# Delta heads of a hybrid decoder layer: order of decays, products, triangle and projections around the triangular inverse

## The chip, the cores and the metric

One core of a Trainium2 chip runs the whole program in one launch. The metric is device time in microseconds. The kernel before took 3432.81 us in the median of three runs (3431.79 to 3434.91).

## What is computed

The program is one inference step of one decoder layer, in float32: a SwiGLU block, a mixer with two branches, and a second SwiGLU block, for a prompt of 1024 tokens and for 8 sample sequences of 4 tokens (32 rows). Branch A is differential attention, branch B a gated DeltaNet. The change lies in branch B. Its core, by head, in chunks:

```python
gc = jnp.cumsum(g.reshape(B, H, n, C), axis=-1)
decay = jnp.exp(jnp.where(incl, gc[..., :, None] - gc[..., None, :], -jnp.inf))
kb = k * beta[..., None]
lower = jnp.where(strict, jnp.einsum('bhncd,bhnmd->bhncm', kb, k) * decay, 0.0)
sol = lax.linalg.triangular_solve(jnp.eye(C, dtype=q.dtype) + lower, rhs, left_side=True, lower=True)
qk = jnp.einsum('bhncd,bhnmd->bhncm', q, k) * decay
q_dec = q * jnp.exp(gc)[..., None]
# then per chunk:
v_new = u_i - w_i @ S
o_i = qd_i @ S + qk_i @ v_new
S = S * gt_i + kd_i.T @ v_new
```

Ahead of this, q, k and v are projected from the normed input, go through a causal convolution of width 4 and SiLU, and q and k are scaled to length one. Behind it, each output row is normed and multiplied by silu(z).

## The kernel before, in words

`delta_heads` (L1132) does branch B for 8 heads of 128 columns. It uses chunks of 128 tokens: 8 tiles of 128 tokens and one of the 32 sample rows (tile 8, called TT). Five instruction streams are written by hand, one per engine, each with its own function `head(h)`; semaphores join them. The order of the code is the order of the work on each engine. The heads run one after another, and the first, the inner and the last are the same code with small differences. The last head has no next head to project for: its "q" unit projects z, its other units project attention's output through the first columns of `w_a_out`, and its z units land in `acc_early`.

**Projections.** `piece(h, kind, c, i, of)` (L1984) is one third (352 columns) of a projection with 1024 inputs: 24 matmuls, as weights and inputs are split in a high and a low part and three of the products are kept. `i, of` cuts a piece in parts. The units of a head are q, z, k, v in this order; q, k and v are those of the next head, z of this one. ACT moves each piece out of PSUM in `take` (L1372), and makes the high part of weights in `high` (L1368); DVE makes the low part in `low` (L1592). `gather` (L1596) and three `product` (L1617) are the convolution on DVE, `silus` (L1409) its SiLU on ACT. PSUM banks 0 and 1 serve the pieces in turn.

**A head on TensorE**, in order: transposes of q and k by tile (`token`), with thirds of the last v piece between them and the transposes of the output rows of the head before (`out_rows`, L2054); piece q 0; `grams` 0 to 3 (L2091), which give k times q and k times k of each tile in banks 2 to 5; pieces q 1 and q 2; gram 4; piece z 0; then the inverse. This goes level by level, up to blocks of 128: in each level 1 to 5 the P products (L2126, in the fifth L2129) of two halves of four tiles, a filling `between(k)`, the R products (L2140), and a second filling. A filling is a sixth of a z piece, four matmuls. For levels up to 4 each P or R group is 64 matmuls of 32x32. Level 6 (`p_last`, `r_last`, L2150 to L2162) is 64x64. After it come value and key products and the scan over the 8 tiles (L2250 to L2261), filled with the k and v pieces.

**What feeds the inverse.** DVE takes the distances of the cumulative gates (`distances`, L1721; gc comes by DMA into `lo_t`, `load_gc` L1312). ACT takes their exponentials, from `qk_t` into `lo_t` (L1494). POOL multiplies by the triangle, from `lo_t` into `qk_t` (L1893). DVE multiplies by the grams in `products(t)` (L1732): first `lo_t`, the lower matrix (L1738), then `qk_t` (L1740), tile by tile. ACT cuts the 32x32 diagonal blocks into `lo_d` (L1504), POOL masks them by level (`masks`, L1897: L1906, L1909, L1913), DVE transposes (`base`, L1771) and TensorE begins. In each level ACT moves P out of PSUM (`moves`, L1512), DVE subtracts R (`update`, L1781) and transposes (`turned`). POOL writes the small blocks into the large matrix in `put` (L1915) and makes kp, scaled q (L1936) and kd ahead of it.

**Norm of the output rows** of the head before: ACT `out_root` (L1447), DVE `row_norm` (L1631), transposes on TensorE, `gate_rows` (L1640) with silu(z). The lengths of q and k: ACT `square`, DVE `sums` (L1703), ACT root (L1487), DVE `scale_columns` (L1708).

## Time and profile before

| | |
|---|---|
| median of three runs | 3432.81 us |
| the profiled execution | 3437.1 us, span of the core 3435.4 us |
| mean granted TensorE clock | 0.984 of full |
| TensorE (PE) busy | 96% |
| its weight loads (PEld) | 91% |
| DVE, ACT, POOL busy | 54%, 42%, 20% |
| DMA | 112 GB/s in the mean |
| the delta heads | from about 1668 to 2424 us |

PE is TensorE, DVE the vector engine, ACT the scalar engine, POOL GpSimd, SP the queue that issues most DMAs. A row of a timeline gives the start, the duration, the engine and line, what is written and read, how many were merged (x), and in brackets how long the engine was idle before it and which instruction ended that. "issue" is idle time in which the engine waited for nothing that the profile shows. PEclk is the clock that TensorE was granted; it has two levels, 1.2 GHz (0.50) and 2.4 GHz (1.00). Matmuls are pipelined, and their ends are modelled.

### The profile page before, as it was taken

Reading aid. Unit: us, or ns where it says so; the run is one execution under the profiler, and the core shown is the slowest. Engines: PE = TensorE matmul, PEld = TensorE weight load, DVE = VectorE, ACT = ScalarE, POOL = GpSimd, SP = SyncE. Lnnn points to the kernel's source line nnn. Section 1 sums busy time; section 2 is a strip of 40 time slices with the busy share of each in tenths; the row PEclk is TensorE's granted clock in tenths of the full one; section 3 lists DMA queues with packets and bytes.
Section 4 is the critical chain, followed back from the end, with each engine's and each line's share of the span. In section 5 each row is a group of like instructions: output and inputs, shape, how many; then the busy total and the mean of one; then the engine's idle time right before and its main releaser. Section 6 shows DMA issues by size and latency. Waiting matters only on the chain. (4 is left out here: it accounts for less than half of the span.)

```text
span 3435.4 us, 70539 instructions
## 1 busy us (share of the span) xinstructions
PE 3314.3 (96%) x28074; PEld 3136.1 (91%) x28074; DVE 1868.7 (54%) x3332; ACT 1459.7 (42%) x3057; POOL 696.4 (20%) x645
## 2 busy tenths in 40 slices
PE   7999999998999999999999999998999899999998
PEld 7999999997888888877788989988999899999998
DVE  6655565764555455544445555554441865556555
ACT  5222235555555555443344444444323722223444
POOL 2323310102122222000022222222001333221000
PEclk9999999999999999999999999999999999999999
DMA  5222236732222222389311111114522322224664
GB/s 165 75 78 84 82 121 218 234 124 70 69 69 69 70 69 69 121 305 379 106 42 44 52 51 52 52 51 130 164 81 75 119 81 82 75 75 147 201 195 141
DMA packets 351893, 385.45 MB, mean 112 GB/s; under 512 B 22492, under 2 KB 259110, under 8 KB 351422
## 3 DMA queue, kind: packets, MB, share of 16 engines
q1 hardware_dynamic: 341606, 347.78, 32.4%
q0 software_dynamic: 9888, 32.88, 2.7%
q8 instruction: 227, 3.72, 0.5%
q14 instruction: 88, 0.72, 0.1%
q10 hardware_dynamic: 84, 0.35, 0.0%
HBM read 305.53 MB, written 75.40 MB: 111 GB/s over the span
## 5 line engine op out<-in xcount | busy, mean ns | idle before, releaser
L673 PE MATMUL ps<-p_hi,w_hi 128*128 128x352 f32 x912 | 304.5, 334 | 2.3 <-PEq L123 1.4
L673 PE MATMUL ps<-p_hi,w_lo 128*128 128x352 f32 x912 | 294.1, 322 | 0.0
L673 PE MATMUL ps<-p_lo,w_hi 128*128 128x352 f32 x912 | 293.4, 322 | 0.0
L1999 PE MATMUL ps<-p_hi,w_hi 128*128 128x352 f32 x840 | 285.6, 340 | 0.0
L1999 PE MATMUL ps<-p_lo,w_hi 128*128 128x352 f32 x840 | 281.9, 336 | 0.2 <-issue 0.2
L1999 PE MATMUL ps<-p_hi,w_lo 128*128 128x352 f32 x840 | 280.8, 334 | 0.0
L673 PEld LDWEIGHTS ps<-p_hi,w_hi 128*128 128x128 f32 x912 | 172.2, 189 | 4.1 <-issue 1.7
L2840 PE MATMUL ps<-op_hid_hi,w_hi 128*128 128x384 f32 (+1 forms) x528 | 170.8, 324 | 4.1 <-DVE w_lo L2515 2.3
L2840 PE MATMUL ps<-f_hid_hi,w_hi 128*128 128x352 f32 x528 | 171.3, 325 | 1.6 <-DVE w_lo L2515 1.5
L673 PEld LDWEIGHTS ps<-p_lo,w_hi 128*128 128x128 f32 x912 | 172.6, 189 | 0.0
L673 PEld LDWEIGHTS ps<-p_hi,w_lo 128*128 128x128 f32 x912 | 171.7, 188 | 0.0
L2840 PE MATMUL ps<-f_hid_lo,w_hi 128*128 128x352 f32 x528 | 169.8, 322 | 0.0
L2840 PE MATMUL ps<-f_hid_hi,w_lo 128*128 128x352 f32 x528 | 169.7, 321 | 0.0
L2840 PE MATMUL ps<-op_hid_hi,w_lo 128*128 128x384 f32 (+1 forms) x528 | 169.4, 321 | 0.0
L2840 PE MATMUL ps<-op_hid_lo,w_hi 128*128 128x384 f32 (+1 forms) x528 | 169.3, 321 | 0.0
L1999 PEld LDWEIGHTS ps<-p_lo,w_hi 128*128 128x128 f32 x840 | 161.4, 192 | 2.6 <-issue 0.7
L1999 PEld LDWEIGHTS ps<-p_hi,w_hi 128*128 128x128 f32 x840 | 161.0, 192 | 2.6
L1999 PEld LDWEIGHTS ps<-p_hi,w_lo 128*128 128x128 f32 x840 | 161.3, 192 | 1.0
L2515 DVE TENSOR_TENSOR w_lo<-w_raw,w_hi 128x512 fp32r<-128x512 f32 x136 | 100.6, 747 | 87.2 <-ACT w_hi L2511 86.9
L414 ACT ACTIVATE at_prob<-ps,at_nmax 128x256 f32<-128x256 f32 (+7 forms) x128 | 94.4, 739 | 81.2 <-DVE at_nmax L520 79.5
L2511 ACT CAST w_hi<-w_raw 128x512 fp32r<-128x512 f32 x136 | 83.7, 619 | 106.2 <-PE ps L2840 106.0
L347 ACT ACTIVATE at_rotx<-ps 32x352 f32<-32x352 f32 x192 | 87.5, 456 | 89.1 <-DVE at_cosx L468 55.0
(698 smaller groups left out, 10354.8 us busy)
## 6 DMA issues: line engine op xcount, KB each, us to landing
w_raw<-in_ffn_w_out_dram SPq DMA_DIRECT2D x136, 256.0 KB, 3.4
w_raw<-in_w_in_dram SPq DMA_DIRECT2D x67, 512.0 KB, 4.0
sa_v<-in_cache_v_dram SPq DMA_DIRECT2D x120, 256.0 KB, 6.7
w_raw<-in_ffn_w_in_dram SPq DMA_DIRECT2D x48, 512.0 KB, 5.1
sa_k<-in_cache_k_dram SPq DMA_DIRECT2D x72, 256.0 KB, 5.5
f_s<-in_ffn_w_out_dram SPq DMA_DIRECT2D x64, 256.0 KB, 3.5
pair_s<-in_ffn_w_out_dram SPq DMA_DIRECT2D x64, 256.0 KB, 3.4
d_hid<-f_gb SPq DMA_DIRECT2D x44, 264.0 KB, 2.1
```

Of the source, the lines that this page charges most:

```text
L347: ins = nc.scalar.mul(dst, src, HD ** -0.5 if kind == "q" else 1.0)
L414: nc.scalar.activation(pr[:, i % 2, a, 0:(i + 1) * P], m.ps[:, 2 + 2 * a:4 + 2 * a, :].rearrange("p b k -> p (b k)")[:, 0:(i + 1) * P], AC ...
L673: mm = nc.tensor.matmul(m.ps[:, bank, 0:CH], a[:, k, w], b[:, f, cols(c)], start=(f == 0 and i == 0), stop=(f == KT - 1 and i == 2))
L1999: mm = nc.tensor.matmul(m.ps[:, (k + c) % 2, 0:CH], a[:, k, f * P:(f + 1) * P], x[:, f, cols(c)], start=(j == 0), stop=(j == len(terms) - 1))
L2511: nc.scalar.copy(unit_slot(u, False), unit_raw(u)).then_inc(e.out_hi, 1)
L2515: nc.vector.tensor_tensor(unit_slot(u, True), unit_raw(u), unit_slot(u, False).bitcast(F32), ALU.subtract).then_inc(e.out_lo, 1)
L2840: mm = nc.tensor.matmul(m.ps[:, bank, 0:hi - lo], unit_slot(u, low_part)[:, o * P:(o + 1) * P], y[:, k, 0:hi - lo], start=(k == 0 and n == ...
```

## The change

- **Decays in place.** ACT's exponentials are written over `qk_t`; `lo_t` gets its first value from the key products. POOL's triangle is applied to `qk_t` alone, behind the query products, and stands in POOL's order after `put`. TensorE waits for it ahead of the scan.
- **Exp of q.** gc for q's scale has a load of its own into `q_t` (`load_gq`), at the start of a head on SP; ACT's Exp of `q_t` is in place and stands after the cuts.
- **Products split.** `products(t)` becomes `key_key(t)` for all eight tiles, then `key_query(t)` for all eight.
- **DVE's order.** The first distances come before `row_norm`, all three sums before `gate_rows`; `gather` and `low` of z come after `base(0)`, the last convolution product goes into level 1, and in the last head `row_low` is spread further back.
- **ACT's order.** `out_root` comes after the second copy of a tile; `high` of z and the take of q's second piece after the cuts; the takes of q 2, z 0 and z 1 into levels 2, 3 and 5; in the last head the Silu of z into level 4.
- **TensorE's order.** z 0 leaves its place before the inverse, of q 2 only the first third stays there. The other two thirds are the fillings 0 and 1, and the nine thirds of z are fillings 2 to 10: eight matmuls each. Filling 11 goes. The wait for z_done moves from gram 2 to gram 3.

```diff
@@ -1150,8 +1150,8 @@
             sem(n) for n in ("staged", "kp", "kd", "km", "eg", "q_scaled"))
-        gc_in, diff_done, dist_done, decay_done, tri_done, gq_mm, low_done, qk_done = (
-            sem(n) for n in ("gc_in", "diff", "dist", "decay", "tri", "gq_mm", "low", "qk"))
+        gc_in, gq_in, diff_done, dist_done, decay_done, tri_done, gq_mm, low_done, qk_done = (
+            sem(n) for n in ("gc_in", "gq_in", "diff", "dist", "decay", "tri", "gq_mm", "low", "qk"))
         g_rows_mm, g_rows_moved, gc_out, o_eps = (sem(n) for n in ("g_rows_mm", "g_rows_moved", "gc_out", "o_eps"))
@@ -1314,6 +1314,11 @@
 
+            def load_gq(x):
+                wait(sp, o_mm, TT * x)
+                sp.dma_start(q_t[:, :], gc_dram[bass.ds(x, 1), :].to_broadcast([P, T])).then_inc(gq_in, 16)
             def first():
@@ -1325,6 +1330,8 @@
 
+                if not (isinstance(h, int) and h == 0):
+                    load_gq(h)
                 wait(sp, state_out, 32 * h)
@@ -1332,6 +1339,7 @@
                     load_gc(0)
+                    load_gq(0)
                     sp.wait_ge(s_low, 1)
@@ -1470,30 +1478,24 @@
 
-                if not (isinstance(h, int) and h == 0):
-                    out_root(h - 1)
                 for t in range(NT):
                     token(t)
+                    if t == 1 and not (isinstance(h, int) and h == 0):
+                        out_root(h - 1)
                     if t == 3:
...
                 square(2)
-                n, k = unit(before(h), "v")
-                if exists(n + 2):
-                    high(n + 2, k)
                 act.wait_ge(sum_sq, 3 * h + 3)
                 nc.scalar.activation(ssq[:, 1, :, 1], ssq[:, 0, :, 1], ACT.Sqrt, bias=m.cst[:, C_EPS:C_EPS + 1]).then_inc(rooted, 1)
-                act.wait_ge(gc_in, 16 * h + 16)
-                nc.scalar.activation(q_t[:, :], lo_flat[:, 0:T], ACT.Exp).then_inc(eg_done, 1)
-                act.wait_ge(eg_done, h + 1)
                 for x in range(3):
...
                     act.wait_ge(dist_done, 3 * h + x + 1)
-                    nc.scalar.activation(lo_t[0:n, 4 * x:4 * x + k, 0:n], qk_t[0:n, 4 * x:4 * x + k, 0:n], ACT.Exp).then_inc(decay_done, 1)
+                    d = qk_t[0:n, 4 * x:4 * x + k, 0:n]
+                    nc.scalar.activation(d, d, ACT.Exp).then_inc(decay_done, 1)
                 take(h, "q", 0)
-                take(h, "q", 1)
                 for x in range(2):
@@ -1502,12 +1504,12 @@
                         nc.scalar.copy(lo_d[rows, tiles, :], lo_t[rows, tiles, rows]).then_inc(cut_done, 1)
-                take(h, "q", 2)
-                if not more:
-                    act.wait_ge(out_done, 16 * h)
-                    act.wait_ge(taken, 3 * unit(h, "q")[0] + 3)
-                    nc.scalar.activation(zs[:, :], xc[:, 0, 0:T], ACT.Silu).then_inc(z_silu, 1)
-                take(h, "z", 0, weights=False)
+                n, k = unit(before(h), "v")
+                if exists(n + 2):
+                    high(n + 2, k)
+                take(h, "q", 1)
+                act.wait_ge(gq_in, 16 * h + 16)
+                nc.scalar.activation(q_t[:, :], q_t[:, :], ACT.Exp).then_inc(eg_done, 1)
 
@@ -1524,13 +1526,19 @@
                     if lev == 2:
+                        take(h, "q", 2)
                         act.wait_ge(t_mm_s, h + 1)
...
                         nc.scalar.copy(tt_s[:, :], m.ps[0:NS, 2, NS:2 * NS]).then_inc(t_moved_s, 1)
-                    if lev == 4:
+                    if lev == 3:
+                        take(h, "z", 0, weights=False)
+                    if lev == 4 and not more:
+                        act.wait_ge(out_done, 16 * h)
+                        act.wait_ge(taken, 3 * unit(h, "q")[0] + 3)
+                        nc.scalar.activation(zs[:, :], xc[:, 0, 0:T], ACT.Silu).then_inc(z_silu, 1)
+                    if lev == 5:
                         take(h, "z", 1, weights=False)
-                    if lev == 5:
                         silus(h, 2)
@@ -1729,44 +1737,49 @@
 
-                def products(t):
+                def gram(t):
                     n, _ = tile(t)
-                    v = m.ps[0:n, gram_bank(t // 2), (t % 2) * 256:(t % 2) * 256 + 256].rearrange("p (k d) -> p k d", d=P)
+                    return m.ps[0:n, gram_bank(t // 2), (t % 2) * 256:(t % 2) * 256 + 256].rearrange("p (k d) -> p k d", d=P)[:, :, 0:n]
+                def key_key(t):
+                    n, _ = tile(t)
                     dve.wait_ge(gq_mm, 5 * h + t // 2 + 1)
                     dve.wait_ge(scales, 4 * h + 3)
-                    dve.wait_ge(tri_done, 3 * h + t // 4 + 1)
-                    nc.vector.scalar_tensor_tensor(out=lo_t[0:n, t, 0:n], in0=v[:, 1, 0:n], scalar=sc[0:n, BP, t:t + 1], in1=lo_t[0:n, t, 0:n],
+                    dve.wait_ge(decay_done, 3 * h + t // 4 + 1)
+                    nc.vector.scalar_tensor_tensor(out=lo_t[0:n, t, 0:n], in0=gram(t)[:, 1, :], scalar=sc[0:n, BP, t:t + 1], in1=qk_t[0:n, t, 0:n],
                                                    op0=ALU.mult, op1=ALU.mult).then_inc(low_done, 1)
-                    nc.vector.tensor_tensor(qk_t[0:n, t, 0:n], v[:, 0, 0:n], qk_t[0:n, t, 0:n], ALU.mult).then_inc(qk_done, 1)
-
+                def key_query(t):
+                    n, _ = tile(t)
+                    dve.wait_ge(low_done, NT * h + t + 1)
+                    nc.vector.tensor_tensor(qk_t[0:n, t, 0:n], gram(t)[:, 0, :], qk_t[0:n, t, 0:n], ALU.mult).then_inc(qk_done, 1)
+                wait(dve, kp_done, h)
+                wait(dve, kd_done, h)
+                wait(dve, s_done, TT * h)
+                nc.vector.tensor_scalar(col[:, :, :], m.cols[:, bass.ds(h, 1), :, :].rearrange("p o k t -> p (o k) t"), 1.0, None, ALU.mult).then_inc(staged, 1)
+                dve.wait_ge(staged, h + 1)
+                distances(0)
                 if inner:
...
                         row_norm(x, h - 1)
-
-                wait(dve, kp_done, h)
-                wait(dve, kd_done, h)
-                nc.vector.tensor_scalar(col[:, :, :], m.cols[:, bass.ds(h, 1), :, :].rearrange("p o k t -> p (o k) t"), 1.0, None, ALU.mult).then_inc(staged, 1)
-                dve.wait_ge(staged, h + 1)
-                distances(0)
-                sums(0)
                 distances(1)
                 distances(2)
+                sums(0)
+                sums(1)
+                sums(2)
                 if inner:
                     gate_rows(0, h - 1)
+                scale_columns()
+                if inner:
                     gate_rows(1, h - 1)
                     gate_rows(2, h - 1)
-                sums(1)
-                sums(2)
-                scale_columns()
-                n, k = unit(h, "z")
-                low(n, k)
-                gather(h, 2)
                 for t in range(TT):
-                    products(t)
-                    if not more and t == 3:
-                        row_low(0)
+                    key_key(t)
+                for t in range(TT):
+                    key_query(t)
                 if not more:
-                    row_low(1)
+                    row_low(0)
 
@@ -1801,20 +1814,25 @@
                 base(0)
+                gather(h, 2)
+                low(*unit(h, "z"))
+                key_key(TT)
+                key_query(TT)
+                base(1)
                 product(h, 2, 1)
-                products(TT)
                 product(h, 2, 2)
                 if not more:
-                    row_low(2)
-                base(1)
-                product(h, 2, 3)
+                    row_low(1)
                 for lev in range(1, LEVELS):
...
                             turned(lev + 1, x)
+                    if lev == 2 and not more:
+                        row_low(2)
                     if lev == 1:
+                        product(h, 2, 3)
                         dve.wait_ge(p_mm_s, 2 * h + 1)
@@ -1888,11 +1906,16 @@
                 wait(pool, s_mm_s, 2 * h)
-                for x in range(2):
-                    pool.wait_ge(decay_done, 3 * h + x + 1)
-                    nc.gpsimd.tensor_tensor(qk_t[:, 4 * x:4 * x + 4, :], lo_t[:, 4 * x:4 * x + 4, :], tri.rearrange("p (o d) -> p o d", o=1).to_broadcast([P, 4, P]), ALU.mult).then_inc(tri_done, 1)
-                pool.wait_ge(decay_done, 3 * h + 3)
-                nc.gpsimd.tensor_tensor(qk_t[0:NS, TT, 0:NS], lo_t[0:NS, TT, 0:NS], m.cst[0:NS, C_TRI4:C_TRI4 + NS], ALU.mult).then_inc(tri_done, 1)
+                def triangle(x):
+                    pool.wait_ge(qk_done, NT * h + 4 * x + PARTS[x][0])
+                    if x < 2:
+                        half = qk_t[:, 4 * x:4 * x + 4, :]
+                        nc.gpsimd.tensor_tensor(half, half, tri.rearrange("p (o d) -> p o d", o=1).to_broadcast([P, 4, P]), ALU.mult).then_inc(tri_done, 1)
+                    else:
+                        part = qk_t[0:NS, TT, 0:NS]
+                        nc.gpsimd.tensor_tensor(part, part, m.cst[0:NS, C_TRI4:C_TRI4 + NS], ALU.mult).then_inc(tri_done, 1)
 
@@ -1944,6 +1967,10 @@
                 put(1)
+                pool.wait_ge(put_done, 8 * h + 8)
+                for x in range(3):
+                    triangle(x)
+                pool.wait_ge(tri_done, 3 * h + 3)
                 pool.wait_ge(kd_done, h + 1)
@@ -2078,9 +2105,9 @@
                         wait(pe, o_moved, TT * h)
-                        if inner:
-                            pe.wait_ge(z_done, 3 * h)
                         wait(pe, tail_moved, h)
+                    if i == 3 and inner:
+                        pe.wait_ge(z_done, 3 * h)
                     if i == 4:
@@ -2103,9 +2130,8 @@
                 piece(h, "q", 1)
-                piece(h, "q", 2)
                 grams(4)
-                piece(h, "z", 0)
+                piece(h, "q", 2, 0, 3)
                 pe.wait_ge(qk_done, NT * h + TT)
@@ -2163,7 +2189,10 @@
                 def between(k):
-                    piece(h, "z", 1 + k // 6, k % 6, 6)
+                    if k < 2:
+                        piece(h, "q", 2, 1 + k, 3)
+                    else:
+                        piece(h, "z", (k - 2) // 3, (k - 2) % 3, 3)
 
@@ -2186,7 +2215,6 @@
                 between(10)
-                between(11)
                 r_last(0)
@@ -2240,6 +2268,7 @@
                 pe.wait_ge(q_scaled, 2 * h + 2)
+                pe.wait_ge(tri_done, 3 * h + 3)
                 for t in range(TT):
```

## Rows read from the trace of the kernel before

**Rows 1.** Busy time of stretches: us, then busy us (instructions) by engine, PEclk, DMA share, GB/s

```profile
1700.00:2400.00 700.00, 674.24 (x8689) 620.55 (x8688) 372.94 (x828) 318.21 (x874) 195.80 (x229) 0.97 0.21 60
```

**Rows 2.** Waits of TensorE, 1660 to 2430 us: total, times, longest

```profile
PE ps L2140 <- issue: 8.6, 12, 1.6
PE ps L2126 <- issue: 5.7, 8, 1.5
...
PE ps L2072 <- ACT dl_tok L1466: 3.4, 9, 0.4
```

**Rows 3.** Timeline of TensorE, an inner head: start, us, line, operation, idle before it

```profile
1976.03 0.71 PE L2072 MATMUL ps<-cst,dl_cs 128*128 128x128 f32 x4 [0.42 <-ACT dl_tok L1466]
...
1990.30 0.32 PE L1999 MATMUL ps<-p_hi,w_hi 128*128 128x352 f32 x1
1990.46 0.32 PE L1999 MATMUL ps<-p_lo,w_hi 128*128 128x352 f32 x1
...
1999.41 1.01 PE L2126 MATMUL ps<-dl_uc,dl_mk 32*32 32x32 f32 x64
...
2003.87 0.39 PE L2126 MATMUL ps<-dl_uc,dl_mk 32*32 32x32 f32 x23 [0.48 <-issue]
...
2007.68 0.58 PE L2126 MATMUL ps<-dl_uc,dl_mk 32*32 32x32 f32 x36 [0.40 <-issue]
```

**Rows 4.** DMA queues, 1998 to 2018 us

```profile
q8 instruction: 5, 0.08, 1.8%
```

**Rows 5.** Timelines of TensorE and POOL, last head, start of the inverse

```profile
2349.69 0.45 PE L2126 MATMUL ps<-dl_uc,dl_mk 32*32 32x32 f32 x32 [0.84 <-POOL dl_mk L1913]
...
2356.43 1.08 PE L2140 MATMUL ps<-dl_lo_d,dl_ttc 32*32 32x32 f32 x64 [5.45 <-ACT dl_lo_d L1516]
...
2355.33 0.24 POOL L1938 TENSOR_TENSOR dl_wq<-dl_q_t,dl_css 128x32 f32<-128x32 f32 x1
```

**Rows 6.** Busy time of one stretch behind a stop, columns as in rows 1

```profile
1746.00:1752.00 6.00, 6.00 (x82) 5.07 (x76) 1.95 (x8) 1.61 (x4) 2.29 (x8) 0.50 0.02 4
```

**Rows 7.** Timeline of TensorE, first head, starts of levels 1 and 2

```profile
1730.71 0.79 PE L2126 MATMUL ps<-dl_uc,dl_mk 32*32 32x32 f32 x64
...
1733.91 0.75 PE L2126 MATMUL ps<-dl_uc,dl_mk 32*32 32x32 f32 x64
```

**Rows 8.** Timelines of DVE and then ACT, the same inner head

```profile
1982.19 1.57 DVE L1646 SCALAR_TENSOR_TENSOR dl_zs<-ps,gain,dl_zs 128x512 f32<-128x512 f32 x3
...
1986.39 1.22 DVE L1594 TENSOR_TENSOR w_lo<-w_raw,w_hi 128x1024 fp32r<-128x1024 f32 x1
...
1990.19 0.35 DVE L1738 SCALAR_TENSOR_TENSOR dl_lo_t<-ps,dl_sc,dl_lo_t 128x128 f32<-128x128 f32 x1 [1.55 <-POOL dl_qk_t L1893]
...
1994.64 2.11 DVE L1617 SCALAR_TENSOR_TENSOR dl_cs<-dl_xc,conv_weight,dl_cs 128x1080 f32<-128x1080 f32 x1
...
1996.93 1.32 DVE L1617 SCALAR_TENSOR_TENSOR dl_cs<-dl_xc,conv_weight,dl_cs 128x1080 f32<-128x1080 f32 x1
...
1985.25 0.30 ACT L1487 ACTIVATE dl_ssq<-dl_ssq,cst 128x9 f32<-128x9 f32 x1 [2.05 <-DVE dl_ssq L1706]
1985.57 1.28 ACT L1489 ACT_TABLE_LOAD   x1
1986.86 1.09 ACT L1489 ACTIVATE dl_q_t<-dl_lo_t 128x1056 f32<-128x1056 f32 x1
...
1991.95 1.26 ACT L1504 COPY dl_lo_d<-dl_lo_t 32x128 f32<-32x128 f32 x4
```

**Rows 9.** Timeline of POOL, the same inner head

```profile
1988.78 2.54 POOL L1893 TENSOR_TENSOR dl_qk_t<-dl_lo_t,cst 128x512 f32<-128x512 f32 x2 [3.75 <-ACT dl_lo_t L1494]
...
1993.37 0.47 POOL L1906 TENSOR_TENSOR dl_mk<-dl_lo_d,cst 128x128 f32<-128x128 f32 x1 [1.84 <-ACT dl_lo_d L1504]
...
1995.56 1.51 POOL L1906 TENSOR_TENSOR dl_mk<-dl_lo_d,cst 128x128 f32<-128x128 f32 x1
...
1998.54 1.28 POOL L1913 TENSOR_TENSOR dl_mk<-dl_lo_d,cst 128x512 f32<-128x512 f32 x1
```

## The prediction

> **What bounds the kernel now.** I read the busy time by stretches first, then the waits of TensorE, then the timeline of TensorE over whole heads, and last the other engines around one stop. The change touches only the delta heads, from 1668 to 2424 us. Between 1700 and 2400 us TensorE is busy 674.24 of 700 us, DVE 372.94 and ACT 318.21 [rows 1]: TensorE is the bound, and only what stops it, or slows its clock, can be won. A projection matmul is issued every 0.16 us, though its modelled span is 0.32 [rows 3], so an idle time of TensorE understates a stop by about 0.16 us.
>
> Four things stop it. First, "issue" inside the groups of 32x32 matmuls of the inverse: 8.6 us in 12 stops at L2140 and 5.7 in 8 at L2126 [rows 2]. The stops fall in the middle of a group [rows 3]: 23 matmuls of a group are left at 2003.87 us, 36 at 2007.68. Counted in the timeline, 126 matmuls lie between these two points, each with its weight load: no semaphore sits there. The DMA view shows an instruction queue that fetched 5 packets, 0.08 MB, in the 20 us around them [rows 4]: 16 KB every 4.0 us, and the stops end 3.81 us apart. So the dense part of the inverse runs out of fetched instructions. Second, the transposes of the third tile wait in every inner head for ACT's copies: 3.4 us in 9 stops [rows 2]. Third, the last head: TensorE stands 0.84 us for POOL's masks and 5.45 us for ACT's first move of level 1 [rows 5]. ACT is there itself waiting, in `take` of z, for POOL's scaled q, which ends at 2355.33 + 0.24 us [rows 5]. Fourth, the clock: from 1746 to 1752 us it is granted at 0.50, that is 1.2 of 2.4 GHz [rows 6], after an issue stop of 1.5 us, the longest at L2126 [rows 2].
>
> **The change, part by part.** No TensorE work is added or removed; all of it is order.
>
> *Eight matmuls between levels instead of four.* A level without a stop lasts 1733.91 - 1730.71 = 3.20 us [rows 7]; it issues 64 + 8 + 64 matmuls and one or two small ones, near 275 instructions with weight loads. The 252 between two fetch points are gone in 2.9 us, while a fetch takes 3.8 at best: 0.9 us short each. With 8 more matmuls a level lasts 3.20 + 8 x 0.16 = 4.48 us for some 292 instructions, so 252 last 3.9 us on average: supply and use are even. They are even only on average, since a stretch with one filling and two groups still takes about 2.9. I therefore keep a third of the stops. Now they cost 8.6 + 5.7 us and 20 x 0.16 = 17.5 us; two thirds, 11.7 us, go. Bounds: all (-17.5) to none (0).
>
> *The last head.* Take of z moves from before level 1 to level 3, and the full Silu of z to level 4. The wait for scaled q then falls two levels (9 us) later than now, while POOL's work moves only with the last convolution product. So 5.45 + 0.16 goes, and the 0.84 + 0.16 is counted under the masks below: -5.6 us.
>
> *Root of the output rows after two copies.* ACT copies tiles 0 and 1 before the table load. The stop of 0.42 + 0.16 us [rows 3] goes, but ACT's chain to the next copies is as long as before, so tile 6 catches part of it. I take -0.3 for seven heads, -2 us; bounds -4 and 0. `row_norm` now follows distances(0), which end about when the root does: free.
>
> *The path to the inverse.* Now: root of the sums at 1985.25 us, behind three gate_rows (1.57 us) and distances; Exp of q_t 1.09, three decays, POOL's triangle 2.54, first key product at 1990.19 [rows 8, 9]. After: the sums come ahead of gate_rows, so the root is at about 1983.2. A table load (1.28) follows and decay 0 ends near 1985.5. gate_rows and the scale columns end near 1985.6. Key products alone, at most 8 x 0.35 [rows 8], end by 1988.4. ACT cuts the first half by 1988.3 (1.26 a half, [rows 8]) and the second by 1989.7. POOL's first masks start at 1988.4 instead of 1993.37; they took 1995.56 - 1993.37 = 2.2 us [rows 9], so the second half starts at 1990.6.
>
> TensorE comes sooner too: 40 matmuls (two thirds of q's last piece, z's first) leave the stretch ahead of the inverse, 6.4 us, and the token gain is 0.3. So it comes to its first 32x32 group at 1999.41 - 6.7 = 1992.7 and to the second half at 1993.1. The price of the second masks is the open one. Undisturbed they take 2.2 us: ready at 1992.8, no stop. Now they take from 1995.56 to 1998.54 + 1.28, 4.3 us [rows 9], because L1906 lasts 1.51 instead of 0.47 us while DVE runs L1617, and L1617 itself 2.11 instead of 1.32 [rows 8, 9]. That gives 1994.9, a stop of 1.8 us. After the change DVE runs at this point gather (a tensor_scalar), low of z (1.22 us, [rows 8]), then products: not L1617 alone. No row shows POOL beside those two. I take 1.2 us, nearer the contended end since something long always runs on DVE; bounds 0 and 1.8, and up to 2.5 if POOL's small masks for the 32 sample rows are late as well. Eight heads: +9.6 us. In the last head this replaces the 1.0 of today: +8.6.
>
> A rule on this: the Trainium skill (SBUF — State Buffer, "SBUF: two separate sides") says that GpSimd and a DVE instruction with two SBUF inputs, or in a 2-port mode, hold a shared port pair exclusively for the whole instruction. The lengthened L1906 and L1617 agree. By it, low of z and gather block POOL like L1617, the stop is the full 1.8 and the whole sum 4.8 us smaller, 3425.
>
> *The rest.* POOL's triangle (2.54 + 0.24 us) moves behind the puts, where POOL idles before km: hidden, and TensorE's new wait for it comes some 10 us later. If that cover were gone it would cost up to 2.8 a head. load_gq adds one broadcast load of gc per head on SP, ahead of the state load and of k's and v's weights; Exp of q_t wants it 15 us after its issue: free. The same low of z now comes at about 1991 instead of 1986.39 [rows 8], and the load of v's weights waits for it on SP, with state and k already issued and load_gc due only after the inverse: free. Silu's table load moves between levels 2 and 3, where ACT only makes two short moves a level: free. The wait for z_done moves from grams(2) to grams(3), which TensorE reaches at about 1986, when gate_rows end: free to 0.3 us. Exp of q_t (1.09), high of z and a take of q sit on ACT between the cuts and the first move: 2.6 us in a gap of 3.4. Behind products 1 and 2 on DVE now waits update of level 1, and product 3 behind that; POOL's kp waits for product 3, scaled q for kp, and both are wanted only after the inverse, or at level 3 in the last head: free.
>
> *Clock.* Fewer long stops, but a new one of 1.2 us per head. The stretch at 1746 us costs 6 x 0.5 = 3 us; I take -2, bounds -8 and +5.
>
> **Sum**: -11.7 - 5.6 - 2 + 8.6 - 2 = -12.7 us. The profiled execution took 3437.1 us (span 3435.4), 4.3 above the median of 3432.81; against the median I forecast 3420.
>
> **Rivals.** (1) *The masks are in time*: DVE's short instructions do not hold POOL, no stop at the start: -12.7 - 8.6 = -21, with all fetch stops gone -27: 3406 to 3412. For it: 2.2 us undisturbed [rows 9]. Against: what L1906 shows. Chance 0.22.
> (2) *The stops move but stay*: spacing the groups only shifts the stops within the inverse. Then the 11.7 is not won and the sum is -1: 3432, no change, so the edit does not do what it says. Against: the first level, entered with fetched instructions after slow matmuls, has no stop [rows 7]; it is the rate of use that runs them dry. Chance 0.16.
> (3) *Slower: the inverse starts before its masks.* TensorE arrives 6.7 us sooner, and the chain ACT root, key products, cuts, masks must keep up. The other terms win 11.7 + 5.6 + 2 + 2 = 21.3 us, and 1.0 of such a stop is paid today. So it turns slower when the stop passes 22.3 / 8 = 2.8 us a head, the second masks ready at 1995.9; with 4 us a head it is +9.7, 3442. The place is L2126 <- POOL L1913. For it: that very wait exists in the last head [rows 5]. Against: it needs 1 us on top of the full contention. Chance 0.10.
> My forecast, 3413 to 3427: 0.52.
>
> **How the numbers follow.** 0.2%, 6.9 us, is about what a measurement of this kernel can tell from no change: below 3426 is faster. Case 1 and nearly all of the forecast's case lie there: 0.70. Same: rival 2 and an edge of mine, 0.20. Slower 0.10. The range goes from rival 1 with a better clock to rival 2: 3404 to 3433.
>
> **What would show it.** An inner head gets shorter by 1 us or more. Issue stops at L2140 and L2126 fall below 6 us together. The 5.45 at L2140 is gone. A wait of about 1 us per head appears at the first group of the inverse, for POOL's masks. The first key product comes 9.6 us behind the transposes of the third tile (1976.03, [rows 3]), where it now comes 14.2 behind. Wrong: issue stops of 14 us as now; start waits of 3 us; a wait on the triangle ahead of the state scan; half-clock stretches after each start stop.

## The result, and the profile after

The change made the kernel faster by 23 us: 3410.85 us in the median of four runs (3409.11 to 3417.86) against 3433.86 of the kernel before in its four (3431.79 to 3435.46), a ratio of 0.993 (0.9912 to 0.9948). That is outside the 0.2% which the prediction called measurable. The profiled execution of after took 3417.86 us, 7 above its own median and the longest of the four, with a span of 3416.2; its mean granted clock is 0.987, before it was 0.984. The forecast of 3420 had the sign right and the time within its range, but little over half of the gain (12.8 us of 23). Its inner bounds, 3413 to 3427 us at a chance of 0.52, were missed by 2 us. What follows looks for the rest.

A line number of before is higher in the kernel after: L1999 is now L2026 (projections), L2126 and L2140 are L2152 and L2166 (P and R products), L2072 is L2099 (token transposes), L1906, L1909 and L1913 are L1929, L1932 and L1936 (POOL's masks), L1738 is L1749 (key products), L1594 is L1602 (`low`).

**How much, and in which heads.** Timelines of TensorE, the first 32x32 group of the inverse in the last four heads of before, and in five heads of after (start, us, line, what is written and read, count):

```profile
2088.44 0.45 PE L2126 MATMUL ps<-dl_uc,dl_mk 32*32 32x32 f32 x32
...
2174.49 0.45 PE L2126 MATMUL ps<-dl_uc,dl_mk 32*32 32x32 f32 x32
...
2260.60 0.59 PE L2126 MATMUL ps<-dl_uc,dl_mk 32*32 32x32 f32 x39
...
2348.39 0.45 PE L2126 MATMUL ps<-dl_uc,dl_mk 32*32 32x32 f32 x32
```

```profile
1729.71 0.46 PE L2152 MATMUL ps<-dl_uc,dl_mk 32*32 32x32 f32 x32
...
2070.55 0.45 PE L2152 MATMUL ps<-dl_uc,dl_mk 32*32 32x32 f32 x32
...
2155.49 0.45 PE L2152 MATMUL ps<-dl_uc,dl_mk 32*32 32x32 f32 x32
...
2239.82 0.45 PE L2152 MATMUL ps<-dl_uc,dl_mk 32*32 32x32 f32 x32
...
2326.51 0.45 PE L2152 MATMUL ps<-dl_uc,dl_mk 32*32 32x32 f32 x32
```

From the first head (1730.71, [rows 7]) to the last is seven heads: 617.7 us before, 596.8 after, so 88.2 and 85.3 us a head, 20.9 us in all. But two heads of before, between 2088.44 and 2260.60, took only 86.05 and 86.11. They have the fewest stops (1.7 and 1.3 us, where the other five have 2.0 to 3.1), and the full clock. Busy time by stretches, three of before and three of after (us, then busy us and instructions of PE, PEld, DVE, ACT, POOL, then PEclk, DMA share, GB/s):

```profile
1670.00:1770.00 100.00, 96.46 (x1129) 88.26 (x1128) 48.65 (x108) 47.11 (x100) 22.63 (x26) 0.93 0.16 42
...
2130.00:2220.00 90.00, 88.40 (x1129) 81.82 (x1128) 49.24 (x108) 42.31 (x119) 24.65 (x29) 1.00 0.20 56
...
2310.00:2400.00 90.00, 80.91 (x1057) 74.28 (x1057) 43.24 (x99) 38.94 (x106) 25.20 (x29) 0.94 0.40 128
```

```profile
1670.00:1770.00 100.00, 98.24 (x1181) 90.20 (x1179) 50.78 (x110) 48.12 (x105) 22.97 (x26) 1.00 0.18 48
...
2130.00:2220.00 90.00, 89.30 (x1138) 82.93 (x1138) 52.61 (x113) 41.53 (x118) 25.51 (x30) 1.00 0.21 62
...
2310.00:2400.00 90.00, 84.35 (x1092) 78.27 (x1091) 38.35 (x92) 38.11 (x108) 22.31 (x27) 0.98 0.40 128
```

Of the eight stretches of 90 to 100 us in which the delta heads lie, six of before are granted less than 1.00 and three of after, those at 0.98. With (1 - PEclk) x length x 2 for the time at 1.2 GHz, that is some 39 us before and 11 after. Two more traces of the kernel after, from runs told below, have 18 and 7.

Now the parts. In these seven heads TensorE's idle times, counted head by head in the timeline, fall from 15.6 us in 27 to 5.7 in 12; with 0.16 for each that is 12.3 us of the 20.9, and the other 9 are put down to the clock, since nothing else is left. From the first group of the last head to the last of its projection matmuls it is 72.7 us before and 74.6 after, though 40 matmuls, 6.4 us, moved into this stretch (and out of that ahead of the first head's group, 62.1 and 55.7 us): 4.5 us won, of which 3.1 in idle time and its 0.16 (8.5 us in 4 stops to 5.6 in 3). 20.9 + 4.5 is 25.4 us, the whole difference of the two profiled delta stages (752.5 and 727.1 us): about 15 us are stops, and 10 are left for the clock. The two spans differ by 19.2 us only, as the rest of the program, which the change does not touch, took 6.2 us more in the profiled execution of after.

That the rest is clock can be checked on the other runs. From the delta stage of each trace (first to last projection matmul) take all its stops, with 0.16 us for each, and set what is left beside the time at 1.2 GHz (us):

| kernel | stage | its stops | what is left | at 1.2 GHz |
|---|---|---|---|---|
| before | 752.5 | 30.6 | 721.9 | 39 |
| after | 727.1 | 15.3 | 711.8 | 11 |
| after, once more | 728.5 | 13.9 | 714.6 | 18 |
| after, third time | 724.6 | 14.4 | 710.2 | 7 |
| short fillings | 748.1 | 21.3 | 726.8 | 50 |
| last head alone | 759.6 | 28.5 | 731.1 | 59 |

What is left rises with the time at 1.2 GHz, by 0.42 us for each us of it, on a straight line through these six and the seven other traces of the runs below (correlation 0.99; doubled groups less the 13 us of their added work). The 28 us between before and after are 12 us by this line. Left out of it are the fillings put in alone: 60.9 us of stops, 64 us at 1.2 GHz and 720.4 left, 12 us below the line. Much of that slow time may lie in the stops themselves; that is not shown.

**Stops.** Waits of TensorE in the kernel after (line, what ended them: us, times, longest):

```profile
PE ps L2152 <- POOL dl_mk L1936: 4.5, 7, 0.8
PE ps L2152 <- issue: 4.4, 4, 2.1
...
PE ps L2152 <- DVE dl_uc L1791: 1.7, 1, 1.7
...
PE ps L2099 <- ACT dl_tok L1474: 0.7, 3, 0.3
...
PE ps L2212 <- issue: 0.3, 1, 0.3
...
PE ps L2166 <- issue: 0.2, 1, 0.2
```

Issue stops fell from 14.3 us in 20 [rows 2], or 14.9 in 22 with the two at other lines, to 4.9 in 6, the tokens' from 3.4 in 9 to 0.7 in 3, and a new one for POOL's second masks stands in seven heads. In an inner head, timeline of TensorE (in brackets the idle time before, and what ended it):

```profile
1984.34 0.46 PE L2152 MATMUL ps<-dl_uc,dl_mk 32*32 32x32 f32 x32
1985.38 0.45 PE L2152 MATMUL ps<-dl_uc,dl_mk 32*32 32x32 f32 x32 [0.59 <-POOL dl_mk L1936]
...
1989.53 0.75 PE L2152 MATMUL ps<-dl_uc,dl_mk 32*32 32x32 f32 x64
...
1994.16 0.75 PE L2152 MATMUL ps<-dl_uc,dl_mk 32*32 32x32 f32 x64
...
1998.55 0.94 PE L2152 MATMUL ps<-dl_uc,dl_mk 32*32 32x32 f32 x64
```

A level takes 4.4 to 4.6 us with no issue stop in it, and 5.2 the first, with the stop for the masks; the forecast had 4.48. POOL and DVE ahead of it, same head:

```profile
1979.45 0.46 POOL L1929 TENSOR_TENSOR dl_mk<-dl_lo_d,cst 128x128 f32<-128x128 f32 x1 [1.42 <-ACT dl_lo_d L1506]
...
1980.41 1.31 POOL L1936 TENSOR_TENSOR dl_mk<-dl_lo_d,cst 128x512 f32<-128x512 f32 x1
1981.67 0.47 POOL L1929 TENSOR_TENSOR dl_mk<-dl_lo_d,cst 128x128 f32<-128x128 f32 x1
1982.21 0.81 POOL L1932 TENSOR_TENSOR dl_ttc<-cst,dl_mk 128x128 f32<-128x128 f32 x1
1982.99 2.25 POOL L1936 TENSOR_TENSOR dl_mk<-dl_lo_d,cst 128x512 f32<-128x512 f32 x1
```

```profile
1976.87 1.81 DVE L1749 SCALAR_TENSOR_TENSOR dl_lo_t<-ps,dl_sc,dl_qk_t 128x128 f32<-128x128 f32 x6
...
1979.46 1.66 DVE L1755 TENSOR_TENSOR dl_qk_t<-ps,dl_qk_t 128x128 f32<-128x128 f32 x8
...
1981.90 0.81 DVE L1620 TENSOR_SCALAR dl_cs<-dl_xc,conv_weight 128x1080 f32<-128x1080 f32 x1 [0.15 <-DVE dl_xc L1617]
1982.63 1.47 DVE L1602 TENSOR_TENSOR w_lo<-w_raw,w_hi 128x1024 fp32r<-128x1024 f32 x1
```

L1936 lasts 1.31 us beside `key_query` (L1755) and 2.25 beside `low`; the second masks take 1981.67 to 1985.24, 3.6 us. In the last head two things stand where the 5.45 stood [rows 5]; TensorE's timeline, and then the DMA queues from 2326 to 2346 us:

```profile
2328.67 0.45 PE L2152 MATMUL ps<-dl_uc,dl_mk 32*32 32x32 f32 x32 [1.71 <-DVE dl_uc L1791]
...
2335.35 0.25 PE L2152 MATMUL ps<-dl_uc,dl_mk 32*32 32x32 f32 x4 [1.80 <-issue]
...
2342.09 0.43 PE L2152 MATMUL ps<-dl_uc,dl_mk 32*32 32x32 f32 x26 [2.09 <-issue]
```

```profile
q1 hardware_dynamic: 5304, 6.30, 92.3%
q8 instruction: 3, 0.05, 1.0%
```

While SP's loads of attention's output keep the DMA engines 92% busy, the instruction queue lands 3 packets in 20 us, the first two of them 6.8 us apart. An inner head gets 5 before [rows 4] and 4 after (1984 to 2004 us), at most 4.5 us apart. Each packet itself takes 1.0 to 1.4 us in both places, so the time is lost ahead of it.

### The profile page after: what moved, and what is told of

Same layout as the page of the kernel before. It is cut to its first block and busy times, and to the rows that moved or that the text cites. A ratio compares the mean times of both kernels' runs of the same rounds, so it can differ in the third digit from the quotient of the medians.

```text
span 3416.2 us, 70602 instructions
## 1 busy us (share of the span) xinstructions
PE 3305.6 (97%) x28074; PEld 3128.7 (92%) x28074; DVE 1866.8 (55%) x3332; ACT 1456.8 (43%) x3057; POOL 697.4 (20%) x645
## 5 line engine op out<-in xcount | busy, mean ns | idle before, releaser
L2026 PE MATMUL ps<-p_hi,w_hi 128*128 128x352 f32 x840 | 282.8, 337 | 0.1
L2026 PE MATMUL ps<-p_lo,w_hi 128*128 128x352 f32 x840 | 279.5, 333 | 0.0
L2026 PE MATMUL ps<-p_hi,w_lo 128*128 128x352 f32 x840 | 279.5, 333 | 0.0
L2026 PEld LDWEIGHTS ps<-p_hi,w_hi 128*128 128x128 f32 x840 | 159.5, 190 | 2.6 <-issue 0.4
L2026 PEld LDWEIGHTS ps<-p_lo,w_hi 128*128 128x128 f32 x840 | 159.5, 190 | 1.9
L2026 PEld LDWEIGHTS ps<-p_hi,w_lo 128*128 128x128 f32 x840 | 159.6, 190 | 1.3
```

The source lines that it names most:

```text
L2026: mm = nc.tensor.matmul(m.ps[:, (k + c) % 2, 0:CH], a[:, k, f * P:(f + 1) * P], x[:, f, cols(c)], start=(j == 0), stop=(j == len(terms) - 1))
```

## The experiments

Each time is a median, beside the kernel before on the same chip.

**The fillings alone, taken back.** Ahead of the inverse the kernel after gets whole q 2 and z 0 again, and between levels four matmuls, with ACT's takes to match:

```diff
-                piece(h, "q", 2, 0, 3)
+                piece(h, "q", 2)
+                piece(h, "z", 0)
...
-                    if k < 2:
-                        piece(h, "q", 2, 1 + k, 3)
-                    else:
-                        piece(h, "z", (k - 2) // 3, (k - 2) % 3, 3)
+                    piece(h, "z", 1 + k // 6, k % 6, 6)
```

> The changed kernel with its fillings put back: q's last piece and z's first whole before the inverse, z's other two in sixths, four matmuls between levels; z's first piece is still taken in level 3. Theory (the fetch of instructions sets the stops, and the clock falls behind them): the issue stops in the inverse come back from about 5 to 14 us, half-clock time in the delta heads rises from 14 towards 37 us, and the kernel takes 12 to 20 us more than the changed one, 3423 to 3431 us. Rival 1 (the stops were latency of the decays' chain, cured by the earlier masks): no more than 3 us slower than the changed kernel. Rival 2 (the clock has nothing to do with the stops): 12 us slower, with half-clock time as in the changed kernel. The masks' stop at the start of the inverse is gone in any case, since TensorE comes 6.4 us later: that is worth 6 us back, which is taken into the numbers.

Measured: 3430.91 us (3414.70 to 3440.30, 12 runs) against 3431.46 (23 runs), ratio 0.9986 (0.997 to 1.0002). The waits of TensorE:

```profile
PE ps L2156 <- issue: 9.2, 9, 3.3
...
PE ps L2170 <- issue: 6.3, 10, 1.6
...
PE ps L2159 <- issue: 0.6, 1, 0.6
```

The issue stops are back, 16.1 us in 20, with no wait on the masks, and the gain is gone: all the other parts of the change together, fewer stops for the masks among them, are not shown to be worth anything (the interval leaves them 0 to 10 us). The time is at the upper end of what the theory expected; the trace has 50 us at 1.2 GHz, where 37 were expected. The mean granted clock of its runs is 0.9844, that of before 0.9849, of after 0.9882.

**The last head alone.** The kernel before, with only the last head's takes of z and Silu moved into the levels:

```diff
-                take(h, "z", 0, weights=False)
+                if more:
+                    take(h, "z", 0, weights=False)
...
+                    if lev == 3 and not more:
+                        take(h, "z", 0, weights=False)
```

> The kernel before with one edit: in the last head the take of z's first piece goes to level 3, the Silu of z to level 4 and the take of z's second piece to level 5. Theory: the stop of 5.45 us at the first R products of the last head is gone, the 0.84 us for the masks stays, and the half-clock stretch behind it goes too: 5.6 to 8 us less than the kernel before, 3426 to 3428 us. Rival: the stop only moves, as ACT waits in level 3 for the scaled q or for the table load: 0 to 2 us.

Measured: 3431.18 us (3423.57 to 3447.22, 12 runs), ratio 0.9987 (0.9973 to 1.0001). The 5.45 us for ACT is gone, but TensorE's timeline has a longer one in the same head, where before it had 0.67:

```profile
2366.74 0.78 PE L2131 MATMUL ps<-dl_uc,dl_mk 32*32 32x32 f32 x37 [3.27 <-issue]
```

Without the wait for ACT, TensorE reaches the end of its fetched instructions sooner, in a stretch where the loads fill the DMA engines (a share of 1.01 from 2350 to 2370 us). Issue stops of this head rise from 2.25 us to 4.21. Some 3.5 us less of stops remain, but the head is no shorter in the profile (73.1 us, before 72.7), with more of it at 1.2 GHz. The medians agree with the rival, 0 to 2 us; the interval, 0 to 9 us less, does not exclude the 5.6 of the theory.

**`low` of z behind the second base.** On DVE, nothing else:

```diff
-                low(*unit(h, "z"))
...
+                low(*unit(h, "z"))
```

> The changed kernel with one edit: DVE's low part of z's weights comes behind base(1) instead of before the sample rows' key product. Theory (DVE's instruction with two SBUF inputs holds POOL's masks back, and holds base(1) back itself): the second half of the masks is ready 1.2 us sooner, the stop of 0.6 us at the second half of the first P group goes in every head, in the last head the stop of 1.7 us too, 6 to 8 us less than the changed kernel, 3403 to 3405 us. Rival 1 (the masks take as long beside the next DVE instruction): within 1 us of the changed kernel. Rival 2 (the low part of z's weights is late for TensorE then, or the update of level 1 is): the stop moves to the second filling or to the P products of level 2, and it is slower than the changed kernel by up to 4 us.

Measured: 3408.17 us (3400.87 to 3412.13, 6 runs), ratio 0.9916 (0.9897 to 0.9935): 3 us less than the kernel after, where 6 to 8 were expected. The stops for the masks are gone from all heads, and so are the 1.7 us in the last. POOL, then DVE, in the same inner head:

```profile
1980.59 0.82 POOL L1932 TENSOR_TENSOR dl_ttc<-cst,dl_mk 128x128 f32<-128x128 f32 x1
1981.37 1.31 POOL L1936 TENSOR_TENSOR dl_mk<-dl_lo_d,cst 128x512 f32<-128x512 f32 x1
```

```profile
1980.29 0.81 DVE L1620 TENSOR_SCALAR dl_cs<-dl_xc,conv_weight 128x1080 f32<-128x1080 f32 x1 [0.15 <-DVE dl_xc L1617]
...
1981.93 1.82 DVE L1602 TENSOR_TENSOR w_lo<-w_raw,w_hi 128x1024 fp32r<-128x1024 f32 x1
```

So `low` alone made the 0.94 us of L1936. Here it starts after L1936, and is itself the longer one, 1.82 us in place of 1.47; `gather` makes 0.35 of L1932 (0.46 in the first half), in both kernels.

**The kernel after once more**, on the same chip:

> The changed kernel once more, for a second trace of it and a narrower interval. Theory (its clock is better because the long stops are gone): half-clock time in the delta heads of 10 to 20 us again, median 3409 to 3413 us. Rival (the clock was luck): 25 to 40 us of half clock, median above 3418 us.

Measured: 3411.05 us (3405.76 to 3413.91, 6 runs), ratio 0.9927 (0.9908 to 0.9945), seven mask stops, 4.5 us, and 18 us at 1.2 GHz. The clock of after was not luck.

**The fillings alone, put in.** The kernel before with the new fillings and ACT's takes to match (the diff of the first experiment, the other way round), and the old path to the inverse; the Silu of z and `row_low` of the last head move as in the change:

> The kernel before with the new fillings alone: q's last two thirds and z's first piece go between the levels, eight matmuls each, and ACT's takes go with them; decays, triangle, products and DVE's order stay. Theory: the issue stops fall to about 5 us as in the changed kernel, but TensorE now reaches the inverse 6.4 us sooner, at masks that are no sooner than before, so each of the eight heads stops 5.5 to 6.5 us for POOL's masks: 44 to 52 us of new stops against 10 to 15 us of gain, 3460 to 3475 us, with more half-clock time behind these stops. Rival (the fillings are the whole gain, the decays' chain is hidden): 3410 to 3420 us.

Measured: 3461.38 us (3456.69 to 3464.03, 4 runs) against 3431.16 (11 runs), ratio 1.0082 (1.0061 to 1.0104). Waits of TensorE, and its timeline in one head:

```profile
PE ps L2125 <- POOL dl_mk L1913: 50.4, 16, 3.8
...
PE ps L2125 <- issue: 1.6, 2, 1.0
```

```profile
2003.52 0.45 PE L2125 MATMUL ps<-dl_uc,dl_mk 32*32 32x32 f32 x32 [2.58 <-POOL dl_mk L1913]
...
2007.74 0.65 PE L2125 MATMUL ps<-dl_uc,dl_mk 32*32 32x32 f32 x32 [3.77 <-POOL dl_mk L1913]
```

The fetch stops go here too, but TensorE now stands 6.3 us in every head for the masks. The new fillings and the shorter path to the masks are one change: the first alone loses 30 us, the second alone wins nothing.

**Root of the output rows ahead of all copies again**, in the kernel after:

```diff
+                if not (isinstance(h, int) and h == 0):
+                    out_root(h - 1)
                 for t in range(NT):
                     token(t)
-                    if t == 1 and not (isinstance(h, int) and h == 0):
-                        out_root(h - 1)
```

> The changed kernel with the root of the output rows back ahead of the first two copies. Theory: the stop of 0.42 us (and 0.16 behind it) at the transposes of the third tile is back in seven heads, and the sums behind it are as late as before: 2 to 4 us more than the changed kernel, 3413 to 3415 us. Rival (ACT's chain through the copies is the bound there in both orders): within 1 us of the changed kernel.

Measured: 3410.17 us (3404.09 to 3414.88, 6 runs), ratio 0.9938 (0.9921 to 0.9954). The stops are back, in all nine places:

```profile
PE ps L2099 <- ACT dl_tok L1474: 3.4, 9, 0.4
```

The kernel after stands at 0.9927 and 0.9926 on the two other chips, and on this one the next two runs, which issue the same work as it, at 0.9942 and 0.9935. Against these the stops cost nothing that can be seen; 2 to 4 us, as expected, are not excluded by the first two.

**Empty instructions**, three behind each filling matmul, once in the inverse and once in the scan. The first:

```diff
+                    for _ in range(idle):
+                        pe.nop(nofuse=True)
...
-                        piece(h, "q", 2, 1 + k, 3)
+                        piece(h, "q", 2, 1 + k, 3, idle=3)
```

> The changed kernel with three empty TensorE instructions behind each matmul of the eleven fillings of the inverse, 264 a head, which use instruction fetch and no array time. Theory (the fetch delivers 256 instructions in 3.8 us at best): a level then issues 340 instead of 292 instructions and cannot pass in less than 5.1 us instead of 4.5, so issue stops come back, 15 to 25 us over the eight heads, with half-clock time behind them: 3425 to 3440 us. Rival (stops are something else than fetch): no more than 3 us over the changed kernel, and no issue stops above 6 us.

> Control for the one before: the same 264 empty instructions a head, but behind the matmuls of eleven fillings of the scan, where 256 instructions last 20 us. Theory: no issue stops are added and the time is within 4 us of the changed kernel, 3408 to 3415 us. Rival (an empty instruction costs TensorE its own time): as much slower as the version with them in the inverse.

Measured: 3411.40 (3406.11 to 3412.73) and 3410.72 us (3405.45 to 3415.89), 4 runs each, ratios 0.9942 (0.9921 to 0.9962) and 0.9935 (0.9913 to 0.9958). Neither shows anything: 2112 more instructions would be 8 more packets, but the instruction queue moved 227, in the kernel after 228, so the empty instructions never reached the program that ran. The pair says nothing of either theory, and was done again with real instructions.

**Doubled groups.** In levels 1 to 4 the four matmuls of the first tile of every P and R group are issued twice; the values stay:

```diff
-                            for b in range(4):
+                            for b in (0, 1, 2, 3) * (2 if j == 0 else 1):
...
-                        for b in (range(4) if lev < LAST - 1 else (0, 2)):
+                        for b in ((0, 1, 2, 3) * (2 if j == 0 else 1) if lev < LAST - 1 else (0, 2)):
```

> The kernel after, but in levels 1 to 4 each P and R group issues the four matmuls of its first tile twice, with the same operands into the same place: the values stay, and a level has 32 more 32x32 matmuls (records of the trace) and 32 more weight loads. A group of 64 such matmuls takes 0.7 us beside the fillings, so 32 more cost 0.35 us a level, 11 us over 4 levels of 8 heads. Theory that the rate of instruction fetch stopped TensorE in the inverse: a level goes from about 292 to 356 instructions, and at a packet of 256 instructions per 3.8 to 4.0 us that is 5.3 to 5.6 us against 4.95 of work, so 0.35 to 0.65 us more a level: issue stops rise from about 5 us to 16 us or more, and the time by 22 to 32 us over the kernel after. Rival, that the issue stops have another cause and went with the old order: they stay at 4 to 6 us in a handful, and the time rises by about 11 us.

Measured: 3437.85 us (3433.16 to 3439.95, 10 runs) against 3435.24 of before (17 runs), ratio 1.0004 (0.9991 to 1.0016). The kernel after, run beside it, took 3412.79, so this is +25.1. Waits and timeline of TensorE:

```profile
PE ps L2166 <- issue: 6.2, 8, 2.4
...
PE ps L2152 <- issue: 4.5, 6, 1.6
...
PE ps L2208 <- issue: 0.7, 1, 0.7
```

```profile
1989.61 0.55 PE L2152 MATMUL ps<-dl_uc,dl_mk 32*32 32x32 f32 x40
...
1995.10 0.95 PE L2152 MATMUL ps<-dl_uc,dl_mk 32*32 32x32 f32 x80
...
2005.62 0.79 PE L2152 MATMUL ps<-dl_uc,dl_mk 32*32 32x32 f32 x63
2006.72 0.33 PE L2152 MATMUL ps<-dl_uc,dl_mk 32*32 32x32 f32 x17 [0.31 <-issue]
```

A group of 80 lasts 0.95 us, one of 64 0.75, so the work itself is 0.4 us a level and 13 over all. The issue stops grow from some 4 us to 11.4 in 15 places, fewer than the 16 expected, but they are back with no other change to the order. The 2048 added instructions are 8 packets of 256, and the instruction queue moved 236 in place of 228. In the three levels from 1989.61 to 2005.62, 5.34 us each with 0.51 of a mask stop among them, packets come every 3.6 to 4.1 us, 3.8 in the mean: as often as the stops of before (3.81 us between two). It bears out the theory of fetch in sign and in total; 13 + 7 + 9 x 0.16 is 22 of the 25.

**The best version, and the two small moves together.**

> The kernel after, with low of z behind base of the second half on DVE, and the root of the output rows ahead of all token copies on ACT, as before the change. Theory that short stops of TensorE for ACT's copies cost nothing that can be measured, since two such runs apart gave 2.9 us (low) and 0.9 us (root) less than the kernel after: 3405 to 3409 us, not slower than low alone. Rival, that a stop of 0.4 us per head costs its length and more: 3411 us or above.

> The kernel after with low of z behind base of the second half on DVE, unchanged from the earlier run. Theory that the stop for POOL's second masks is caused by DVE's low of z and worth its 4.5 us in seven heads or somewhat less: the difference to the kernel after stands, 3407 to 3409 us, no stop at the masks in any inner head. Rival, that the 2.9 us between the two medians was scatter: 3410 to 3412 us.

> The kernel after unchanged, to have it beside the other three on the same chip: 3409 to 3412 us in both theories, seven stops of about 0.6 us for POOL's second masks and issue stops of 4 to 5 us in 3 to 6 places.

Measured, side by side: with both 3406.76 us (3398.41 to 3412.36), ratio 0.991 (0.9893 to 0.9927); `low` alone 3408.33 (3403.55 to 3412.43), 0.9918 (0.9903 to 0.9934); the kernel after 3412.79 (3407.04 to 3414.69), 0.9926 (0.9911 to 0.9942); 6 runs each. With `low` moved the medians are 2.9 and 4.5 us below the kernel after, on two chips. The intervals of the ratios overlap, so the size is open; the sign was the same both times. The root in its old place costs nothing here, as 3406.76 is not above 3408.33. The kernel after came 1 us above its expected range.

## Why the prediction was right, and where its size was off

**The bound and its cause held.** The inverse ran out of fetched instructions, and more work per instruction between the groups ended that. The forecast of two thirds, 11.7 us of 17.5, compares with 14.3 us in 20 stops becoming 4.9 in 6: with 0.16 us for each, 17.5 to 5.9, 11.6 won (12.5 with the two stops at other lines). Putting the old fillings back alone brought the stops back, and so did doubled groups in the new order. The Trainium skill (Advanced Engine Details and Errata, "ISA Cache") gives a cache line of instructions as 16 KB, 256 instructions; the packets of 16 KB and the 126 matmuls with their loads between two stops agree. The traces show the cause directly as well. Each of the 22 issue stops of before ends 1.2 to 1.6 us after a packet of the instruction queue has landed: the two of [rows 3], at 2003.87 and 2007.68 us, both 1.44 us after packets that landed at 2002.43 and 2006.24. The same holds for all 20 of the short fillings and all 15 of the doubled groups. Packets come some 4 us apart in the inverse, so stops of another cause would not keep that distance.

**Rival 2 fell** with it: the stops did not move within the inverse, they went.

**The masks.** The step said 1.2 us a head, between 0 and 1.8; measured 0.58 to 0.83 in seven of eight, 4.5 us, with 0.16 each 5.6 in place of 9.6. The start of the first masks, 12.4 us behind the third tile's transposes by the forecast, was at 12.5 (1966.90 to 1979.45), the first key product at 10.0 instead of 9.6. The masks were 3.6 us instead of 4.3, and TensorE came 0.7 later. The Trainium skill (SBUF — State Buffer, "SBUF: two separate sides") has DVE with two SBUF inputs and GpSimd exclude each other for a whole instruction. The trace agrees as to which instruction does it: `low`, with two inputs in SBUF, costs L1936 0.94 us, while `key_query`, which reads PSUM, leaves it at 1.31. By that rule taken in full the sum was to be 4.8 us smaller, 3425; this did not come, since the overlap was only partial. Rival 1, masks in time, was wrong as a cause, but its time (3406 to 3412) is what came: its gain had another source. The kernel with `low` moved is that rival, and is 3 to 4.5 us faster, not the 8.6 it was priced at. Part of it went elsewhere: its traces have issue stops of 4.3 us in 5 and 5.6 in 7, where the kernel after beside them has 3.9 in 3 and 4.1 in 6.

**The last head.** The step took 5.6 us for the wait of ACT. The wait went as said, and the last head gave 4.5 us in the profile together with its share of the fillings. By itself the edit is not shown to be worth anything: an issue stop of 3.27 us stands in that head, and one of 3.31 with short fillings, where before it was 0.67. "Where a stop goes, what is late next" was answered with the masks there; it was the fetch, held up by the loads. In the kernel after 1.7 us for DVE's base, behind a `low` of 2.32 us, comes on top.

**The root after two copies** was put at -2 us. Its stops went, 2.7 us of them, and putting them back cost nothing that can be seen, neither in the kernel after nor in the one with `low` moved.

**The clock is the step that was mis-sized.** The prediction took -2 us, with -8 as the end, from one stretch of 6 us [rows 6]. It never added up the stretches. They come to 39 us before and 11 after; what the stops leave of the 25.4 us is 10, and the line through thirteen traces gives 12. By the prediction's own price, half of the slow time, it would be 14. The runs say the same without a profile: over the 23 runs of before that stand beside the short fillings a straight line through time and mean granted clock falls by 2.5 us for each 0.001, over the 12 of the short fillings by 3.3, and the means of before and after (0.9849 and 0.9882) are 0.0033 apart: 8 to 11 us. Put in place of the -2, with the other terms as measured, the sum is -11.6 for the fetch, -4.7 for the last head (0.84 and 5.45 us in two stops become 1.71 in one), +5.6 for the masks and -10 for the clock: -21 us, and at most 4 more if the stops of the tokens count in full; -23 was measured. The forecast priced the masks too high by some 3 us and the clock too low by 8; both made it too cautious, so neither error hid the other.

**Which stops the clock answers to is open.** The short fillings, with 16 us of issue stops, run at 0.9844; the fillings put in alone, with 50 us of mask stops, at 0.9828; but doubled groups, with 11 us, at 0.9877, and the nine stops of up to 0.4 us for ACT left it at 0.9893. Fewer and shorter stops go with a higher clock, but not by their sum alone: `low` moved has the fewest stops of all, and ran at 0.9870 and 0.9877. In the profiled execution of before, the four heads whose longest stop was 0.95 us or more each have a stretch at 1.2 GHz, and of the three with shorter ones one has. In that of after two inner heads with 0.59 and 0.65 us have one, and the first, with 0.83, has none. No run here sets one stop of a chosen length by itself.

## What to carry to other kernels

Before small stops of TensorE are priced by their length, add up the half-clock time of all stretches, and compare units of work at full clock with the others; afterwards take the stops out of the stage and see whether the rest follows that time. Here the stops were worth 15 us and the clock another 10. Where dense small matmuls outrun the fetch, spread large ones between them, and shorten the path that then becomes late in the same change, since either alone gained nothing or lost. When a wait is removed in a stretch where DMA is full, look at the fetch of instructions next: in the last head of three kernels here it stopped TensorE for 1.8 to 3.3 us at a time. To tell a fetch stop from another, set its end beside the landings of the instruction queue.

## What was not expected of the hardware

- Instruction fetch is later where DMA is full: packets of 16 KB up to 6.8 us apart and issue stops of 1.8 to 3.3 us where the DMA engines are 92% busy and more, against 3.4 to 4.7 us apart and stops of 0.2 to 1.5 us in the inverse of the other heads. No run takes the loads away by themselves.
- TensorE goes on 1.2 to 1.6 us after the packet that it stood for has landed, at all 57 issue stops of before, of the short fillings and of the doubled groups.
- Stops of TensorE of up to 0.4 us before the token transposes, 3.4 us in nine places against 0.7 in three, could be put in and taken out with no change of the time that can be seen (3410.17 and, on the same chip with the three alone, 3411.40 and 3410.72 us; 3406.76 and 3408.33 us).
- Runs of one kernel on one chip spread by up to 25 us (3414.70 to 3440.30, short fillings), and most of it goes with the mean granted clock of each run, 0.987 to 0.981.
